# The skip term of a state-space kernel made by ScalarE, with reordered splits and loads in the stages behind it

## The reference

```python
def finish(y, xs, z):
    b, n = xs.shape[:2]
    y = y + xs.astype(jnp.float32) * d_skip.astype(jnp.float32)[:, None]
    y = (y.reshape(b, n, SSD_DI) * jax.nn.silu(z.astype(jnp.float32)))
    y = y.reshape(b, n, SSD_GROUPS, SSD_DI // SSD_GROUPS)
    y = y * lax.rsqrt(jnp.mean(y * y, axis=-1, keepdims=True) + RMS_EPS)
    y = (y.reshape(b, n, SSD_DI) * norm_g.astype(jnp.float32)).astype(xs.dtype)
    return y @ w_out
```

## Time and profile before

| what | value |
| --- | --- |
| median of 3 runs | 2197.6 us (2196.13 to 2199.01) |
| the profiled execution | 2196.73 us |
| its span, first to last instruction | 2194.8 us |
| its mean granted PE clock | 0.972 of full speed |
| PE busy | 2044.9 us |
| DVE, ACT, POOL busy | 1340.1, 1115.3, 421.2 us |

### The profile page before, as it was taken

How to read it: one execution, slowest core, us unless ns; L and a number is a source line. 1 busy time by engine, 2 the same in 40 slices (tenths; PEclk the granted TensorE clock), 3 DMA queues, 4 the chain that set the end, 5 groups by cost and what they waited for, 6 DMA issues and landing times. The chain is left out here.

```text
span 2194.8 us, 34774 instructions
## 1 busy us (share of the span) xinstructions
PE 2044.9 (93%) x12274; PEld 1685.9 (77%) x12274; DVE 1340.1 (61%) x3091; ACT 1115.3 (51%) x2750; POOL 421.2 (19%) x382
## 2 busy tenths in 40 slices
PE   4899999999999999999786999889999999999797
PEld 2588888888888888888665888778878878878576
DVE  4475868768695877869594533435555555555553
ACT  4344848566574857667472322324444444444441
POOL 1012112121212212121342333211011011110300
PEclk9799999999999999999998999999999999999799
DMA  9522322221221322223254443321221221221432
GB/s 371 224 68 72 97 79 97 72 81 68 86 95 60 97 67 87 68 86 101 86 174 144 150 152 119 92 59 49 78 68 49 78 68 49 78 68 43 153 88 84
DMA packets 133192, 214.15 MB, mean 98 GB/s; under 512 B 31164, under 2 KB 91660, under 8 KB 130972
## 3 DMA queue, kind: packets, MB, share of 16 engines
q1 hardware_dynamic: 121500, 169.97, 24.8%
q10 hardware_dynamic: 11520, 41.95, 5.8%
HBM read 180.94 MB, written 28.69 MB: 96 GB/s over the span
## 5 line engine op out<-in xcount | busy, mean ns | idle before, releaser
L422 PE MATMUL h_bank<-h_h_hi,h_whi 128*128 128x512 f32 (+1 forms) x1792 | 684.0, 382 | 8.4 <-ACT at_vv L2268 5.3
L424 PE MATMUL h_bank<-h_h_hi,h_wlo 128*128 128x512 f32 (+1 forms) x1792 | 648.8, 362 | 0.0
L423 PE MATMUL h_bank<-h_h_lo,h_whi 128*128 128x512 f32 (+1 forms) x1792 | 646.9, 361 | 0.0
L422 PEld LDWEIGHTS h_bank<-h_h_hi,h_whi 128*128 128x128 f32 x1792 | 341.2, 190 | 63.3 <-issue 12.9
L424 PEld LDWEIGHTS h_bank<-h_h_hi,h_wlo 128*128 128x128 f32 x1792 | 340.1, 190 | 54.2
L423 PEld LDWEIGHTS h_bank<-h_h_lo,h_whi 128*128 128x128 f32 x1792 | 341.7, 191 | 45.4
L1099 POOL TENSOR_TENSOR sg_xdb<-sg_X,sg_tab 128x256 f32<-128x256 f32 x144 | 125.5, 872 | 616.6 <-ACT sg_X L966 402.2
L955 ACT ACTIVATE sg_S<-sg_rowb,sg_tab 128x128 f32<-128x128 f32 x640 | 195.4, 389 | 20.8 <-DMA sg_rowb<-crows 17.9
L2382 POOL TENSOR_TENSOR h_wlo<-h_wr,h_whi 128x1024 fp32r<-128x1024 f32 x31 | 73.8, 2381 | 537.8 <-ACT h_whi L2253 537.8
L1229 DVE TENSOR_TENSOR sg_hb<-sg_hb,h_bank 128x256 f32<-128x256 f32 x72 | 30.3, 421 | 186.5 <-PE h_bank L732 186.4
L2164 PE MATMUL h_bank<-at_ident,at_pm 128*128 128x128 f32 x640 | 104.7, 279 | 22.0 <-ACT at_ptr L2306 22.0
(11 more groups left out here) (294 smaller groups left out, 3908.3 us busy)
## 6 DMA issues: line engine op xcount, KB each, us to landing
sg_rowb<-crows ACTq DMA_DIRECT2D x80, 512.0 KB, 3.7
h_wr<-in_w_ssd SPq DMA_DIRECT2D x48, 512.0 KB, 3.3
fs_w<-in_ada_w SPq DMA_DIRECT2D x16, 1024.0 KB, 8.3
h_wr<-in_w_na SPq DMA_DIRECT2D x32, 512.0 KB, 3.4
at_bias<-bt SPq DMA_DIRECT2D x256, 64.0 KB, 2.3
md_yr<-y SPq DMA_DIRECT2D x34, 256.0 KB, 3.0
fs_w<-in_ada_w SPq DMA_DIRECT2D x16, 512.0 KB, 7.8
y<-sg_Z SPq DMA_DIRECT2D x16, 512.0 KB, 5.5
```

The lines of the kernel that those rows point to most:

```text
L422: pe.matmul(out, w_hi[:, k, :], h_hi[:, k, t0:t0 + n], start=(k == 0), stop=False)
L423: pe.matmul(out, w_hi[:, k, :], h_lo[:, k, t0:t0 + n], start=False, stop=False)
L424: x = pe.matmul(out, w_lo[:, k, :], h_hi[:, k, t0:t0 + n], start=False, stop=(k == KT - 1))
```

## The change

It does these things:

- The skip term `xD` of chunk c+1 is made by ACT behind `decays(g, c + 1)`, as four scaled copies of 64 columns, with a wait for `yoS`. POOL's product L1127 goes, and so does its wait; POOL keeps `xdb`.
- In the last group POOL scales y parts 0 and 1 in the two slots before `FIRST`; the low halves stay where they were. DVE's low half of the output weights moves ahead of the convolution, `gated` and `nearer`.
- In the middle stage the y parts 6 and 7 are split at step 11 and loaded behind the weights of step 12; loads of the other parts shift likewise. The loads for the gates go from step 12 to step 15, DVE's gates from behind step 14 to behind step 15.
- In attention the first `windows` goes behind the second weight load of pair 1.
- ACT's `take` keeps the eviction; the weight split and the tanh become `follow`, behind the exponential and the copy of the transposed values.

```diff
+        scale_slot = [FIRST - 2, FIRST - 1] + part_slot[2:]
...
+            def skip_term(g, c):
+
+                n = g * NCH + c
+                if n >= 2:
+                    act.wait_ge(yoS, n - 1)
+                for k in range(HPG):
+                    x = act.activation(xD[:, n % 2, k * HD:(k + 1) * HD], xth(g, c)[:, k // 2, k % 2, :], ACT.Copy,
+                                       scale=dsk[:, g * HPG + k:g * HPG + k + 1])
+                x.then_inc(xDs, 1)
...
                     if -1 <= c < NCH - 1:
                         decays(g, c + 1)
+                        skip_term(g, c + 1)
...
                     scaled((c + 1) % 2, g, c, 0)
-                n = g * NCH + c
-                if n >= 2:
-                    pool.wait_ge(yoS, n - 1)
-                pool.tensor_tensor(heads(xD[:, n % 2, :].rearrange("p (h c) -> p h c", c=HD)), xth(g, c),
-                                   heads(dsk[:, g * HPG:(g + 1) * HPG].unsqueeze(2)
-                                         .to_broadcast([P, HPG, HD])), ALU.mult).then_inc(xDs, 1)
...
                     for i in range(len(oparts)):
-                        if g == G - 1 and part_slot[i] == s:
+                        if g == G - 1 and scale_slot[i] == s:
                             pool.wait_ge(oyl[i % 2], 32 * (i // 2 + 1))
...
+                    for i in range(len(oparts)):
+                        if g == G - 1 and part_slot[i] == s:
                             pool.wait_ge(oyh, i + 1)
...
                         times_decay(g, c + 1)
+                    if g == G - 1 and c >= 0:
+                        if c == 0:
+                            dve.wait_ge(ong, 16)
+                        dve.wait_ge(owh, c + 1)
+                        dve.scalar_tensor_tensor(ow[1][:, c, :], ow_raw[c % RO], ng[:, c:c + 1], ow[0][:, c, :].bitcast(F32),
+                                                 ALU.mult, ALU.subtract).then_inc(owls, 1)
                     if at(step, 1) is not None:
                         conv(at(step, 1))
...
-        y_with = {10: (6, 7), 12: (8,), 13: (9,), 15: (10, 11)}
+        y_with = {11: (6, 7), 12: (8,), 13: (9,), 15: (10, 11)}
+        y_load_with = {12: (6, 7), 13: (8,), 14: (9,), 15: (10, 11)}
...
-                for i in y_with.get(k, ()):
+                for i in y_load_with.get(k, ()):
                     load_y(i)
-                if k == K0 + 2:
+                if k == K0 + 5:
                     sp.dma_start(pg, a["post_g"][0].partition_broadcast(P)).then_inc(gl, 16)
...
-                if k == K0 + 4:
+                if k == kt - 1:
                     dve.wait_ge(gl, 48)
...
-                    if i == 0 and p:
+                    if i == 0 and p >= 2:
                         windows(p - 1)
+                    if i == 1 and p == 1:
+                        windows(0)
...
                 x.then_inc(pev, 1)
+
+            def follow(q):
+
+
+                p, i, kd, b = units[q]
+                w = p * len(KINDS) + i
                 if b == ublocks[kd][0] and w + 1 < PR * len(KINDS):
                     split(w + 1)
...
                 out_weight(n, 0)
+                for q in stretch(n, 0):
+                    follow(q)
                 exps(n, 1)
                 for q in stretch(n, 1):
                     take(q)
                 if n:
                     keep_turned(n - 1, 1)
                 out_weight(n, 1)
+                for q in stretch(n, 1):
+                    follow(q)
                 for q in stretch(n, 2):
                     take(q)
+                    follow(q)
```

More of the change, by code:

```diff
@@ L1394, in _ @@
                         split_lo(q // NBL + 1)
-                    if g == G - 1 and c >= 0:
-                        if c == 0:
-                            dve.wait_ge(ong, 16)
-                        dve.wait_ge(owh, c + 1)
-                        dve.scalar_tensor_tensor(ow[1][:, c, :], ow_raw[c % RO], ng[:, c:c + 1], ow[0][:, c, :].bitcast(F32),
-                                                 ALU.mult, ALU.subtract).then_inc(owls, 1)
             variances(G - 1)
```

## The result

The changed kernel takes 2240.5 us (median of 4 executions, 2233.99 to 2243.01) against 2198.0 for the kernel before in the same comparison: a ratio of 1.0197 [1.0177, 1.0217], 42.5 us slower. The forecast was 2219, or +21, with 2231 as its upper end: the sign was right, and the size forecast is half of the measured one. The profiled execution after took 2241.85 us (span 2240.1, mean granted clock 0.963; before 0.972), so 45.3 us of span are to be explained.

What follows compares the result with a forecast made beforehand. PE, busy 93% of the span, was taken as the bound, so only its idling counts. Terms 27.2 + 2 + 0.5 - 6.5 - 7.2 + 5.5 = +21.5 gave a 2219 us median; range 2209 to 2229, widened by rivals to 2203 to 2231.

Steps and rivals of the forecast that it cites:

- Clock: State-space groups, slot 1: PE's longer waits bring some work at the 1.2 GHz level, +2 us (0 to 10).
- The middle stage: Weights load first, gates last: step 15 ends 7.9 us sooner, second turn waits +1.4; together -6.5 us (-9 to -1).
- Copies: Groups, slots 1, 3 and 6: ACT's skip copies delay PE 0.97 us in 28 places, +27.2 us (16.5 to 33).
- Rival 4: Groups: slack in ACT's queue covers the skip copies, so the kernel is faster, 2192 at no cost; chance 0.08.
- Rival 2: Groups: the clock falls in slot 1 of every group, +8 us, 2227; chance 0.14.
- POOL: POOL loses 80 operations of 808 ns mean; PE hardly waits for it, so 0, or up to 5 us.
- rival 3: Last group: without POOL's nine products DVE is relieved, its loop turns some 0.5 us faster, 2214; chance 0.07.
- Last group: Early POOL scales gain at the first weight, the early low half eats it in some eight slots; +0.5 us (-8 to +6).
- Start of attention: The weight load goes ahead of the window copies, so PE's 5.00 us wait and slow work go; -7.2 us (-8 to -4).
- Pairs: Attention: PE's 1.28 us wait goes, but DVE's copy makes its transposes 0.8 us later; +5.5 us over 7 pairs (-9 to +7).
- Rival 1: Attention pairs: POOL does not hold DVE's silu once both shift, so 9.0 us are won, 2204.5; chance 0.16.
- the dearer copy: Groups: a chunk's four skip copies cost 1.18 us instead of 0.97, +6 us, used for the range's upper end.

Runs made afterwards that it cites:

- e5: The changed kernel with ACT's four skip-term copies moved from behind the decays to behind the square; 2215.0 us, ratio 1.0088 to before.
- e1: The kernel before with the skip term moved from POOL to ACT and nothing else; 2235.7 us, ratio 1.0167 to before.
- e6: The changed kernel with DVE's low half of the output weights back at the end of its slot in the last group; 2234.0 us, ratio 1.0171 to before.
- e10: The changed kernel with modulated(0) made ahead of the y parts of the middle stage's second turn, on ACT and DVE; 2230.4 us, ratio 1.0150 to before.
- e7: The changed kernel with DVE's silu of the g units moved behind its copy of the transposed values; 2227.2 us, ratio 1.0145 to before.
- e3: The changed kernel with gate loads back behind step 12's weights and DVE's gates behind step 14's low half; 2233.4 us, ratio 1.0153 to before.
- e9: The kernel before plus early POOL scales, early DVE low half, later windows, ACT's `follow`, and g-unit silu behind the transposed-value copy; 2180.5 us, ratio 0.9914.

## Why the prediction was wrong

The steps that failed are the terms "Clock" and "The middle stage", and the pairs' term in that same clock.

- **Copies: right.** "0.97 us", 28 places, "+27.2": measured 0.96 and 26.2 us. Place and price came from rows, and e5 shows the place to be the cause. Rival 4 (covered) is out.
- **Clock: the step that failed in the groups.** I took "+2", on one pair of rows of another stage, and gave the fall in every group a rival's 0.14. Rival 2 is what happened: the long slot behind slot 1 ran slow in all seven groups, and took 11.6 us in two of them, 9.4 us more than before in all. The trace of before already held the answer: in three of its seven groups (0, 3 and 4) the long slot takes 10.2 us behind waits of 1.9, 1.19 and 1.26 us. I had read the waits of slot 1 and not the slot behind them.
- **POOL, and rival 3: nothing**, as forecast. No run shows a gain from the products that POOL lost; in e1, where they go alone, the last group keeps its length.
- **Last group: sign right, small.** The early scales gained more than I said (4.0 where they come alone, against 2.7), the early low half cost 4.2 beside the copies (e6) against the "+2.2" that I had for "some eight slots".
- **Middle stage: wrong by 10.5 us**, the largest miss. Step 15 ended 3.9 us sooner and not 7.9. "Landing 4 us" was 7.7, the waits of steps 12 to 14 add up to 8.3 us and not 6.3, and the products between them ran slower than I had let them, another 2 us. "+1.4" at the second turn was the graver one: I worked it out from the normed tile and overlooked that the turn also waits for `modulated(0)`, which both engines make behind two y parts. In the trace before, that tile was ready only 0.15 us ahead of the turn, and the late gates made it 1.2 us later still: 3.9 - 0.15 + 1.2 is the wait of 4.9 us. Behind it PE runs slow: from this turn to the next are 22.8 us, before 20.0. All of the 3.9 was lost there; e10 shows the cause. The miss is 4.0 (step 15), 3.5 (the wait) and 2.8 (the clock), 10.3 of the 10.5.
- **Start of attention: right**, -6.9 for -7.2.
- **Pairs: mechanism right, size off by the clock.** "0.8 later than before" is 0.75 in the three undisturbed pairs. Four pairs lose 1.55 us more behind the wait, where the products run at the 1.2 GHz level. Together 7 x 0.75 + 4 x 1.55 = 11.5 where I had 5.5. Rival 1 failed because the silu is held by POOL; e7 shows it from the other side.

Together: 7.4 (clock in the groups), 10.5 (middle stage), 6.0 (pairs), 1.0 (last group) and 0.3 (start of attention), less 1.0 for the waits of the groups and 0.6 net in the small rests, are 23.6 of the 23.8 us between the forecast +21.5 and the 45.3 of the span. The upper end was also added up wrongly: 2219 with rival 2 (8) and the dearer copy (6) is 2233, not 2231.

## What to carry to other kernels

Before pricing a longer wait of TensorE, look at the work behind the waits that the trace already has: if it is slow behind some of them, the added waits cost more than their own length, here another 9.4 us on 26.2 in the groups and 6.2 on 5.3 in the pairs. When a wait is taken away, list every semaphore of the instruction that comes next, not only the one named last, for the gain ends at the second latest. And a helper operation that is moved forward in an in-order queue is only free if its inputs are ready there: in e6 they were at the end of the slot, and ahead of gating and minimum they were not.

## What the runs showed of the hardware

**The clock behind a wait.** In 14 traces PE waits in slot 1 of seven groups, then works through one long slot without a gap. Sorted by the wait:

| wait | long slots | at 8.5 to 8.6 us | 10.1 us or more | of these 11 us or more |
| --- | --- | --- | --- | --- |
| 0.64 to 1.11 us | 13 | 13 | 0 | 0 |
| 1.16 to 1.67 us | 29 | 14 | 15 | 0 |
| 1.70 to 2.79 us | 16 | 3 | 13 | 2 |
| 2.84 to 4.72 us | 40 | 0 | 40 | 13 |

The same wait of 1.62 us in attention was followed by products of 2.40 us in four of seven pairs and of 1.31 in three. Over the six traces that have this wait, the products behind it were slow (2.26 to 2.40 us) in 25 of 42 places. A wait of 1.28 us stood in each pair before, and in four other traces, and none of these 35 was followed by slow products. So a wait of some one and a half microseconds cost another 1.6 us about every second time, and one of 2.8 us or more cost it in all 40 places. No run changed the length of one wait alone: the table shows what went with what, and what decides between two waits of the same length stays open. In the trace after, the lower level behind the three kinds of added wait costs 9.4 + 2.8 + 6.2 = 18.4 us, 0.8% of the span, and that is 40% of what the change costs. The Trainium skill (TensorE: Matmul & The Clock Gate, Part 1) puts the penalty of the warm-up ramp at under 1% of a typical kernel's span. Counted over every stretch at the lower level, this trace does not stay under that: PE is busy for 125.3 us at the lower level, and as products take about half as long at the upper one (0.23 us against 0.43 from one product of 512 columns to the next), some 58 us, or 2.6% of the span, is my estimate of what it costs in all. The same working on the 39.7 us more that PE is busy at the lower level after than before gives 18.5 us, which agrees with the 18.4. The amount is too large to leave out of a change of this size.

**POOL beside DVE, by the start.** Late in the middle stage DVE makes four low halves of 1024 columns while POOL makes two. Most traces look like the one after, with three of them in 4.07 us and the fourth by itself; in three (e3, e6 and e9) the four take 9.7 to 10.0 us, and PE's last turn waits 4.4 to 4.7 us instead of 2.1. The kernel after, then e9, each with POOL's two low halves:

```profile
1423.95 4.07 DVE L1826 TENSOR_TENSOR h_h_lo<-md_ht,h_h_hi 128x1024 fp32r<-128x1024 f32 x3 [6.93 <-ACT h_h_hi L1691]
...
1426.85 6.76 POOL L1741 TENSOR_TENSOR h_h_lo<-md_ht,h_h_hi 128x1024 fp32r<-128x1024 f32 x2 [2.18 <-ACT h_h_hi L1691]
```

```profile
1375.77 9.74 DVE L1820 TENSOR_TENSOR h_h_lo<-md_ht,h_h_hi 128x1024 fp32r<-128x1024 f32 x4 [6.92 <-ACT h_h_hi L1685]
...
1378.66 5.76 POOL L1735 TENSOR_TENSOR h_h_lo<-md_ht,h_h_hi 128x1024 fp32r<-128x1024 f32 x2 [2.05 <-ACT h_h_hi L1685]
...
1396.48 1.97 PE L1606 MATMUL h_bank<-md_ident,md_yr 128*128 128x128 f32 x8 [4.42 <-DVE md_yr L1808]
```

The program order is the same in both. The traces differ in who starts first. DVE's third low half starts at 1426.81 in the kernel after and POOL's first 0.04 us later; DVE's takes 1.21 us and POOL's 3.41. In e9 POOL's starts at 1378.66, 0.09 us ahead of DVE's third, which then takes 3.41 us and POOL's 2.42. This holds in all 14 traces: POOL starts 0.09 to 0.35 us ahead in the three slow ones, and between 0.01 us ahead and 0.15 us behind in the eleven others. What shifts the start by a tenth of a microsecond was not tried, and stays open, as does what part of it can be planned for.
